# Two transformer blocks in one kernel: sums of squares paired on GpSimd, another place for four transposes, another order of the heads, wider chunks of one weight

## The reference

```python
def short_conv_branch(b_gate, c_gate, v, conv_w, w_conv_out):   # first block
    z = c_gate * v
    ...                                                         # 3 taps along the sequence
    return (b_gate * y) @ w_conv_out                            # 512 -> 1024

def second_block(x, p, ...):
    h = x
    for i in range(L):                                          # 2 layers
        u = rmsnorm_2(h, norm_mix_pre[i]) @ w_in[i]
        ...
        y_attn = dsa_sparse_attention(q, k, v, qi, ki, wi)      # 8 heads of 64
        y_conv = conformer_conv(u_conv, ...)                    # 31 taps, layernorm, silu, 256x256
        y_pool = multiscale_pool(u_pool, pool_w[i], pool_scale[i])
        mix = concatenate([y_attn, y_conv, y_pool]) @ w_out[i]
        h = h + rmsnorm_2(mix, norm_mix_post[i])
        m = rmsnorm_2(h, norm_mlp_pre[i])
        m = square(relu(m @ w_up[i])) @ w_down[i]               # 1024 -> 4096 -> 1024
        h = h + rmsnorm_2(m, norm_mlp_post[i])
        gate = sigmoid(h @ ple_gate[i])
        h = h + gate * (p[i] @ ple_proj[i])
    return h

def rmsnorm_2(x, g):
    return x * rsqrt(mean(x * x, axis=-1) + 1e-6) * g
```

## Time and profile before

| | before |
|---|---|
| runs, us | 1982.83, 1984.45, 1986.07 |
| the profiled execution, us | 1984.42 |
| its span, us | 1982.6 |
| PE busy | 1940.0 us (98%) in 16060 matmuls |
| DVE busy | 1349.6 us (68%) |
| ACT busy | 997.7 us (50%) |
| POOL busy | 236.8 us (12%) |
| DMA | 329.57 MB, mean 166 GB/s |

### The profile page before, as it was taken

The page is one execution under the profiler, slowest core; times in us unless marked ns, Lnnn a source line. Parts: engine busy times, 40 slices in busy tenths (PEclk is TensorE's granted clock), DMA queues, the critical chain, the costliest instruction groups (busy, mean ns, idle before and its releaser), DMA issues.

```text
span 1982.6 us, 36952 instructions
## 1 busy us (share of the span) xinstructions
PE 1940.0 (98%) x16060; PEld 1921.7 (97%) x16060; DVE 1349.6 (68%) x1608; ACT 997.7 (50%) x1233; POOL 236.8 (12%) x168
## 2 busy tenths in 40 slices
PE   8999999999999999999999999999999999799999
PEld 8999999999999999999999999988999999799998
DVE  6655777775559555787785557885855589676556
ACT  5443545553347444545554336766533366654433
POOL 3000100010002000100010001572100016710000
PEclk9999999999999999999999999999999999899999
DMA  8555454455554655534556554413555443236551
GB/s 272 198 181 182 145 173 161 139 202 191 192 194 152 213 189 181 184 122 148 168 172 207 192 191 158 134 69 128 170 191 188 160 156 108 70 110 231 191 183 52
DMA packets 246533, 329.57 MB, mean 166 GB/s; under 512 B 6246, under 2 KB 218788, under 8 KB 246372
## 3 DMA queue, kind: packets, MB, share of 16 engines
q1 hardware_dynamic: 246018, 326.79, 49.4%
q0 software_dynamic: 96, 0.26, 0.1%
q10 hardware_dynamic: 258, 0.16, 0.0%
HBM read 326.14 MB, written 1.05 MB: 165 GB/s over the span
## 4 chain that ended last, share of the span: by engine, by line
PE 78%; DVE 13%; ACT 4%; POOL 3%; issue 1%; DMA 1%; ACTq 0%; DVEq 0%; POOLq 0%; SPq 0%
PE work L2028 17%; PE work L2029 17%; PE work L2030 17%; PE acc L2030 8%; PE acc L2028 8%; PE acc L2029 8%; DVE w_lo L1312 5%; ACT w_hi L800 2%; POOL fa L747 1%; DVE ra L1325 1%; DVE fa L1751 1%; DVE fa L1357 1%; DVE xl L1346 1%; DVE fa L1908 0%; PE work L2175 0%
## 5 line engine op out<-in xcount | busy, mean ns | idle before, releaser
L1312 DVE TENSOR_TENSOR w_lo<-raw,w_hi 128x2048 fp32r<-128x2048 f32 (+2 forms) x313 | 708.1, 2266 | 107.6 <-ACT w_hi L800 105.4
L2028 PE MATMUL work<-xh,w_hi 128*128 128x256 f32 x2560 | 722.0, 282 | 7.1 <-DVE w_lo L1312 4.9
L2029 PE MATMUL work<-xl,w_hi 128*128 128x256 f32 x2560 | 718.9, 281 | 0.0
L2030 PE MATMUL work<-xh,w_lo 128*128 128x256 f32 x2560 | 717.3, 280 | 0.0
L800 ACT ACTIVATE w_hi<-raw 128x2048 fp32r<-128x2048 f32 (+2 forms) x313 | 577.0, 1851 | 163.4 <-PE work L2030 75.1
L2028 PEld LDWEIGHTS work<-xh,w_hi 128*128 128x128 f32 x2560 | 482.6, 189 | 11.3 <-issue 6.7
L2029 PEld LDWEIGHTS work<-xl,w_hi 128*128 128x128 f32 x2560 | 483.3, 189 | 0.3
L2030 PEld LDWEIGHTS work<-xh,w_lo 128*128 128x128 f32 x2560 | 483.4, 189 | 0.0
L2028 PE MATMUL acc<-ra,w_hi 128*128 128x256 f32 x1352 | 380.1, 281 | 0.0
L2030 PE MATMUL acc<-ra,w_lo 128*128 128x256 f32 x1352 | 379.7, 281 | 0.0
L2029 PE MATMUL acc<-ra,w_hi 128*128 128x256 f32 x1352 | 378.9, 280 | 0.0
(11 more groups left out here) (302 smaller groups left out, 2336.4 us busy)
## 6 DMA issues: line engine op xcount, KB each, us to landing
raw<-in_ffn_w_gu_dram SPq DMA_DIRECT2D x88, 1024.0 KB, 5.1
raw<-in_w_in_dram SPq DMA_DIRECT2D x52, 1024.0 KB, 5.3
raw<-in_ffn_w_down_dram SPq DMA_DIRECT2D x44, 1024.0 KB, 4.8
raw<-in_w_up_dram SPq DMA_DIRECT2D x32, 1024.0 KB, 5.3
raw<-in_w_down_dram SPq DMA_DIRECT2D x32, 1024.0 KB, 4.8
raw<-in_w_mla_out_dram SPq DMA_DIRECT2D x8, 1024.0 KB, 5.3
raw<-in_w_o_dram SPq DMA_DIRECT2D x8, 1024.0 KB, 4.8
raw<-in_w_ple_gate_dram SPq DMA_DIRECT2D x8, 1024.0 KB, 5.0
```

Of the source, the lines that this page charges most:

```text
L1312: v.tensor_tensor(w_lo[:, s, 0:n], raw[:, r, 0:n], w_hi[:, s, 0:n].bitcast(F32), ALU.subtract).then_inc(lo_done.sem, 1)
L2028: pe.matmul(dst, ah, bh, start=start and i == 0, stop=False, skip_group_check=not group)
L2029: pe.matmul(dst, ah, bl, start=False, stop=False, skip_group_check=not group)
L2030: last = pe.matmul(dst, al, bh, start=False, stop=stop and i == len(pairs) - 1, skip_group_check=not group)
```

## The change

1. `w_conv_out` comes in two chunks of 512 columns (128x2048) and no longer in four of 256 (128x1024); the four units d0 to d3 stay, two to a chunk. DVE and ACT split them at two places where there were four.
2. GpSimd gets `row_pairs`: for a bank, it adds the second row of squares to the first (128x256) and signals `pair_sum`. It does so for banks 0 to 2 of the norm after the output product and for all four banks of the norm after the MLP. PE then takes 5 and 4 matmuls by `ones` in place of 8 and 8; after the output product they stand one bank later than before.
3. The unit "p" moves in the list of units from behind the last up unit to before the first. PE's four flips move from the MLP's end to just before the pair up0, up1, which has 28 warm matmuls in place of 36. ACT's and DVE's parts of p move behind the first `hid`.
4. In the norm after the MLP, ACT rounds rows 0 and 1 of h before the copies of proj 2 and 3, and the rest behind them.
5. In the heads of block 2: of the three taps ahead of the first exponentials ACT does one, one after them and the third in hd 2; PE takes `output` of the head before ahead of the accumulate, and the accumulates of `WO2_LOW` behind the mean's sum; DVE splits one chunk in hd 5 in place of hd 4.

```diff
@@ -131,3 +131,3 @@
 out += [("w_uq", 0, 3, hp * 384, 384), ("w_ukv", 0, 2, hp * 512, 512)]
-out += [] if hp else [("w_conv_out", 0, CONV // P, i * 256, 256) for i in range(4)]
+out += [] if hp else [("w_conv_out", 0, CONV // P, i * 512, 512) for i in range(2)]
 out += [("w_in", 0, KD, IN_GM + hp * 256, 256)]
@@ -233,4 +233,4 @@
     names += ["var", ("out", HEADS - 1), "otb", "pw", "mix"]
-    names += [("up", j) for j in range(MLP_STEPS)]
-    names += ["p"] + [("proj", i) for i in range(4)] + [("gate", i) for i in range(4)]
+    names += ["p"] + [("up", j) for j in range(MLP_STEPS)]
+    names += [("proj", i) for i in range(4)] + [("gate", i) for i in range(4)]
     return {n: i for i, n in enumerate(names)}
@@ -726,2 +727,8 @@
 
+    def row_pairs(here, event, n):
+
+        for b in range(n):
+            gp.wait_ge(*sq_ready.at(here, event + b))
+            gp.tensor_tensor(sq[:, 2 * b, :], sq[:, 2 * b, :], sq[:, 2 * b + 1, :], ALU.add).then_inc(pair_sum.sem, 1)
+
     for layer in range(DEPTH):
@@ -777,3 +784,5 @@
             tap(j)
+        row_pairs(here, NB + 1, NB - 1)
         fold(here, 1, 2 * NB + 1, 1 * KD + 5)
+        row_pairs(here, 3 * NB + 1, NB)
 
@@ -970,5 +979,5 @@
             if not hp:
-                for i in range(4):
+                for i in range(2):
                     next_hi(here, D1 + i)
-                c += 4
+                c += 2
             if hp:
@@ -1153,3 +1162,3 @@
         hi_of_unit(here, U2["qt", 1], ("qt", 1), qh[:, 2:4, :], bank2(U2["qt", 1]))
-        some_taps(3)
+        some_taps(1)
 
@@ -1192,3 +1202,3 @@
             if 0 < hd < 6:
-                some_taps(1)
+                some_taps(2 if hd == 2 else 1)
             if hd == 5:
@@ -1239,4 +1249,5 @@
             act.activation(hh[:, j % 2, :, :], hid[:, j % 2, :, :], ACT.Copy).then_inc(hh_ready.sem, 1)
+            if j == 0:
+                hi_of_unit(here, U2["p"], "p", ph[:, :, :], bank2(U2["p"]))
         next_hi(here, down_chunk(MLP_STEPS - 2))
-        hi_of_unit(here, U2["p"], "p", ph[:, :, :], bank2(U2["p"]))
         next_hi(here, M2 + 31)
@@ -1247,2 +1258,4 @@
         for i in range(4):
+            if i == 2:
+                norm_hi(here, 2, None, lambda b: (h_new, NB + b), squares=False, banks=(0,), dst=gh, first=1)
             act.wait_ge(unit_ready.sem, unit_ready.after(here, U2["proj", i]))
@@ -1250,3 +1263,3 @@
                 unit_taken.of(U2["proj", i]), 1)
-        norm_hi(here, 2, None, lambda b: (h_new, NB + b), squares=False, dst=gh, first=1)
+        norm_hi(here, 2, None, lambda b: (h_new, NB + b), squares=False, banks=range(1, NB), dst=gh, first=1)
         next_hi(here, G2)
@@ -1597,4 +1610,5 @@
                     conv_out(i)
-                    next_lo(here, D1 + i)
-                c += 4
+                    if i % 2:
+                        next_lo(here, D1 + i // 2)
+                c += 2
             scaled(here, UE["gm", hp], smla[:, 2 * hp:2 * hp + 2, :])
@@ -1871,5 +1885,4 @@
                 next_lo(here, Q2)
-            if hd == 4:
-                next_lo(here, Q2 + 1)
             if hd == 5:
+                next_lo(here, Q2 + 1)
                 lo_of_unit(here, U2["ota"], "ota", xl[:, 0:2, :], bank2(U2["ota"]), xh[:, 0:2, :])
@@ -1959,4 +1972,4 @@
                 next_lo(here, up_chunk(1))
+                lo_of_unit(here, U2["p"], "p", pl[:, :, :], bank2(U2["p"]), ph[:, :, :])
         next_lo(here, down_chunk(MLP_STEPS - 2))
-        lo_of_unit(here, U2["p"], "p", pl[:, :, :], bank2(U2["p"]), ph[:, :, :])
         next_lo(here, M2 + 31)
@@ -2279,4 +2292,4 @@
                 for i in range(4):
-                    project(here, D1 + i, UE["d", i], depth=CONV // P, x=(yh, yl))
-                c += 4
+                    project(here, D1 + i // 2, UE["d", i], depth=CONV // P, cols=512, x=(yh, yl), first=i % 2 * 2)
+                c += 2
             project(here, c + 2, UE["gm", hp])
@@ -2483,2 +2496,4 @@
                 scores(hd + 2)
+            if hd:
+                output(hd - 1)
             if 1 < hd < 6:
@@ -2489,7 +2504,2 @@
                 accumulate(here, WO2_POOL, rows(6), first=True, banks=(hd - 2,))
-            if hd > 5:
-                pe.wait_ge(*unit_taken.at(here, U2["ota"]))
-                accumulate(here, WO2_LOW, rows(0), banks=(hd - 6,))
-            if hd:
-                output(hd - 1)
             if hd == 0:
@@ -2508,2 +2518,5 @@
                 sum_of("mean", cacc)
+            if hd > 5:
+                pe.wait_ge(*unit_taken.at(here, U2["ota"]))
+                accumulate(here, WO2_LOW, rows(0), banks=(hd - 6,))
         pe.wait_ge(*sq_ready.at(here, NB))
@@ -2525,4 +2538,7 @@
 
-            pe.wait_ge(*sq_ready.at(here, NB + 1 + b))
-            for k in (2 * b, 2 * b + 1):
+            if b < NB - 1:
+                pe.wait_ge(*pair_sum.at(here, b))
+            else:
+                pe.wait_ge(*sq_ready.at(here, NB + 1 + b))
+            for k in (2 * b, 2 * b + 1)[:1 if b < NB - 1 else 2]:
                 last = pe.matmul(bank(U2["mix"])[:, 0:T], ones, sq[:, k, :], start=k == 0, stop=k == KD - 1,
@@ -2533,7 +2549,15 @@
             accumulate(here, WO2_CONV, rows(4), done=0, banks=(b,))
-            if b:
-                mix_sum(b - 1)
+            if b > 1:
+                mix_sum(b - 2)
+        mix_sum(NB - 2)
         mix_sum(NB - 1).then_inc(unit_ready.sem, 1)
 
-        pair(here, M2, (U2["up", 0], U2["up", 1]), normed(here, 1), idle=36)
+        u = U2["p"]
+        free(here, u)
+        pe.wait_ge(prow_full, layer * 16 + (DEPTH * 16 + 16))
+        for k in range(2):
+            for tb in range(TB):
+                last = flip(bank2(u)[:, k, tb * P:tb * P + P], prow[:, tb, k * P:k * P + P])
+        last.then_inc(unit_ready.sem, 1)
+        pair(here, M2, (U2["up", 0], U2["up", 1]), normed(here, 1), idle=28)
         halves(here, up_chunk(2), U2["up", 2], lambda: summed(here, "mlppre", 1))
@@ -2547,9 +2571,2 @@
 
-        u = U2["p"]
-        free(here, u)
...
         pe.wait_ge(hl_ready.sem, hl_ready.after(here, MLP_STEPS - 1))
@@ -2561,3 +2578,6 @@
                 pe.wait_ge(*acc_taken.at(here, NB))
-                summed_by_bank(here, 3 * NB + 1, sums[:, 0, :], sum_ready.event(here, "mlppost"))
+                for b in range(NB):
+                    pe.wait_ge(*pair_sum.at(here, NB - 1 + b))
+                    last = pe.matmul(sums[:, 0, :], ones, sq[:, 2 * b, :], start=b == 0, stop=b == NB - 1)
+                last.then_inc(sum_ready.event(here, "mlppost"), 1)
             project(here, G2, U2["proj", i], depth=2, cols=D, x=(ph, pl), first=2 * i)
```

## The result

| | before | after |
|---|---|---|
| runs, us | 1979.77 to 1986.07, median 1982.83 (5) | 1991.35 to 1993.91, median 1992.65 (5) |
| ratio after to before | | 1.0047, 95% interval 1.0037 to 1.0058 |
| span of the profiled run, us | 1982.6 | 1992.1 |
| PE busy, us | 1940.0 | 1936.5 |
| POOL busy, us | 236.8 | 253.7 |

What follows compares the result with a forecast made beforehand. The prediction took the kernel as bound by TensorE's matmuls, busy 98% of the span. Terms 10.6 + 2.6 - 5.6 + 0 + 2.8 - 5.0 = +5.4 on 1984.4 gave 1990 us, range 1978 to 1999.

Steps and rivals of the forecast that it cites:

- The wait for p: PE before up3, both layers: waits 5.3 us for p's low part on DVE, +10.6 for two layers.
- The clock behind it: PE behind the wait before up3: half clock costs 1.3 per wait (bounds 0 and 1.7), +2.6 for two.
- The norm behind the MLP: MLP's end: p's flips, 8 records and lost time before the gate pair go, -2.8 per layer, -5.6 for two.
- The norm behind the output product: Block 1's conv output product: three matmuls by ones go, but PE waits for GpSimd; 0, bounds -1.3 and +2.0.
- Lone durations: Norm behind the output product: GpSimd adds not slowed, -2.6 in all; part of a rival at about 1983, chance 0.20.
- adds held up at every norm: Both norms: each GpSimd add held up by a w_lo, +1.5 to +2 per norm and layer, 1996; chance 0.12.
- The wide chunks: Rotation: PE 1.9 later in both layers, +3.8; a layer 1 wait goes, -1.0; sum +2.8, bounds 0 and +4.
- The heads: Block 2 heads: waits for exponentials and taps go, POOL still holds the mean; -2.1 and -2.9, sum -5.0.
- The sum: Whole kernel: all terms together +5.4 us, from 1984.4 to 1990.
- The half-clock rival: Behind four new waits of 5 to 7 us: half clock twice as long, +8, 1997 or 1998; chance 0.12.
- The first rival: Heads run at PE's own pace, not held by POOL; some 16 us idle go, 1977; chance 0.13.

Runs made afterwards that it cites:

- two runs: Changed kernel with p's high and low parts ahead of the norm's root and reciprocal: 1977.15 us; changed kernel with p's low part ahead of up4's split: 1987.31 us.

## Why the prediction held, step by step

The sign and the mechanism held: the new wait for p, in both layers, with a half clock behind it, outweighs what the other parts gain. The size held in part. That 1992.65 lies only 2.7 us from the forecast of 1990 owes something to luck: I counted from 1984.4, and the median of five runs of the kernel before is 1982.83. Of the change itself I forecast 5.4 us of 9.3, and in that sum errors of 6.1 one way and 2.6 the other partly cancelled.

- **The wait for p**: forecast 5.3 per layer, 5.18 and 5.16 measured. The step from DVE's order to PE's wait held, nothing in the MLP loop gave it back, and two runs show it (gone, or shorter by just the split).
- **The clock behind it**: forecast 2.6 in all. The offsets give 1.7 and 2.6, 4.3: the term was too small. I had taken 1.3 where one row of before showed 1.7, and had made that one row my upper bound; layer 1 lies above it. The kernel before has longer ones in its heads, which I didn't look for, though the mean clock of 0.91 over 55 us in the earlier trace rows is 5 us lost in each layer, and my one stretch 1.7 of them:

```profile
1345.00:1351.80 6.80, 6.80 (x35) 0.51 0.47 168
1713.70:1720.70 7.00, 7.00 (x36) 0.51 0.49 164
```

- **The norm behind the MLP**: forecast -2.8 per layer. Layer 1: 12.5 - 9.5 = -3.0; layer 0 -3.6 down to the next norm (offset +6.1 at 1625.60), 0.2 of it a shorter wait for GpSimd there. The 8 records give 1.7 of it.
- **The norm behind the output product**: forecast 0; -0.15 by the run with the pair sums alone. Lone durations (-1.3) and adds held up at every norm (+1.5 to 2) are both refuted. Beside that, the rule of the Trainium skill named in the prediction ("SBUF — State Buffer", "Who interferes with whom") gave 0, and the trace agrees with it: the pair sum that met DVE's split took 2.35 us and ended 0.6 us behind the split, the next one took 0.72.
- **The wide chunks**: forecast +2.8, measured +5.1 by the offsets (5.8 - 0.6) and +4.9 by the medians of the part alone. The wait was right, 2.37 us for 2.4. The step that failed is a term left out: I priced the clock behind waits of 5 us and not behind one of 2.4, though the earlier trace rows show it behind 3.64. It costs 1.2 per layer by the offsets.
- **The heads**: forecast -5.0. From first flips to last flips the offset falls by 2.3 and 0.9, the small waits behind them (0.41 and 0.63 in layer 0, of which 0.38 is left, and 0.44 in layer 1) give another 1.1: -4.3; the part alone gave -3.4. The wait before the mean is 5.5 for my 6, by GpSimd as said. The half clock behind it costs 1.6 and 2.8 where I had 1.2 each, 2.0 too little. Against that, `conv_done` comes 5.2 and 5.0 us earlier behind the heads' first flips (4.3 and 5.1 forecast), and the small waits gave 1.1 for 0.8; the single terms don't account for the last tenths.
- **The sum**: forecast +5.4, measured +9.3 by the ratio and +9.5 in the spans. 0.6 of the 9.5 is there ahead of anything that the change touches (in part PE's first wait for a DMA, 5.6 us for 5.2). The terms that were mis-sized are the clock's: 1.7 too little behind p, 2.0 behind the mean, 2.4 left out behind the rotation. The rest came out 2.6 better than forecast: 1.3 in the heads, 0.8 at the MLP's norm, 0.3 at the other norm and 0.3 in the wait for p. The half-clock rival had the mechanism, with a price of 8 on top of the forecast (its four times 2.2 is 8.8) where 3.7 came at its four places; the rotation it didn't name. The first rival (heads at PE's own pace) is refuted: in every kernel with the heads' new order in which PE stood before the mean, GpSimd released it.

Open: what sets the length of a half clock. In the changed kernel the same wait cost 1.7 us in one layer and 2.6 or 2.8 in the other, but it isn't the layer: with p's low part before the split it was 2.9 in layer 0 and 1.5 in layer 1, behind the mean in the heads alone 2.2 and 1.5. Each is one execution, so the terms of the clock above are uncertain by about 1 us at each place.

## What to carry to other kernels

When a buffer's user is moved in front of others, ask which instruction frees it and what stands ahead of that instruction on its engine: that wait and the half clock behind it cost 14.6 us, more than the whole change lost, and moving two instructions ahead of the norm's root and reciprocal gave it back. In this kernel, bound by TensorE, a standstill of 2.4 us and more was nearly always paid for twice, once as idle time and once at half clock, so a wait is best filled with work that has to be done anyway; filler only buys the clock, and only where nothing else sets the next step. Try each part of a bundle alone: here three parts gained some 8 us by their medians (2.2 of them, the first rows', not told from no change), and two lost 5 and 15.

## What the runs showed of the hardware that was not expected

- PE waits of 2.37 and 2.38 us for the rotation were each followed by a half clock; waits of 0.46 at the same place, before, weren't (granted clock 1.00 in 260 to 280). The stretches behind them in the profile after:

```profile
270.40:274.00 3.60, 3.56 (x18) 0.55 0.85 284
883.80:887.20 3.40, 3.39 (x21) 0.71 0.95 306
```

- It isn't certain to come. The profiles of six kernels have this wait of 2.4 us twice each: ten of the twelve have a half clock behind it (1.7 us lost each), two have none. These two, with the wide chunks and p's parts early (wait until 268.96) and with warm matmuls in the wait (until 881.98):

```profile
269.00:273.00 4.00, 4.00 (x34) 1.00 0.77 256
882.00:886.00 4.00, 4.00 (x33) 1.00 0.80 259
```

- In the changed kernel's waits of over 5 us the granted clock fell while PE stood still (0.50 from 1786.5 on, in the wait that ends at 1787.62). In its two waits of 2.4 us it was still whole at the end and fell when PE worked again, at 270.8 (0.4 us behind the wait's end) and at 885.2 (1.4 us).

- A half clock also came with no wait over 0.75 us, among the narrow matmuls of the heads (0.57 in 1691.5 to 1695.5), and with 12 matmuls on zeros per layer ahead of it the profiled execution has none. The two stretches of 6.8 and 7.0 us in the kernel before have no wait over 0.8 us in the 3 us ahead of them either.
- Two GpSimd adds of 128x512 took 4.80 us beside a DVE split, in place of 2.70, and the split 2.81 in place of 2.28: both took longer than apart. The kernel before has it too (two adds, 4.57 us from 1701.48).
